# Down matrices of the expert loop loaded from ScalarE's queue in place of SyncE's

## The reference, cut to what matters

```python
# per layer: 64 experts, each token goes to 8 of them
shared = (silu(xf @ sw1) * (xf @ sw3)) @ sw2
xe = xpad[tok]                                # tokens of expert e
h  = silu(xe @ w1[e]) * (xe @ w3[e])          # w1, w3: 1024 x 256, 1 MB each
y  = (h @ w2[e]) * g[:, None]                 # w2: 256 x 1024, 1 MB
out = out.at[tok].add(y)
```

## Time and profile before

| | |
|---|---|
| time, median of 3 runs | 1429.8 us (1428.21 to 1430.89) |
| the profiled execution | 1428.44 us, of which its span is 1425.9 us |
| TensorE's granted clock, mean | 0.990 |
| busy share of the span | PE 97%, DVE 35%, ACT 24%, POOL 8% |
| HBM read | 459.52 MB |
| DMA queues | q1 (hardware) 452.07 MB, q0 (software, GpSimd's) 8.53 MB |
| expert loop, pairs 2 to 31 | about 225 to 665 us (layer 0) and 930 to 1370 us (layer 1) |

### The profile page before, as it was taken

The page is one execution under the profiler, slowest core; times in us unless marked ns, Lnnn a source line. Parts: engine busy times, 40 slices in busy tenths (PEclk is TensorE's granted clock), DMA queues, the critical chain, the costliest instruction groups (busy, mean ns, idle before and its releaser), DMA issues.

```text
span 1425.9 us, 21714 instructions
## 1 busy us (share of the span) xinstructions
PE 1383.4 (97%) x8662; PEld 852.7 (60%) x8662; DVE 503.5 (35%) x817; ACT 338.4 (24%) x860; POOL 117.7 (8%) x155
## 2 busy tenths in 40 slices
PE   9989999999999999998999999999999999999988
PEld 4555766566665666654497557656666565665543
DVE  1575623333333333334311255232333323333352
ACT  1243232222222222221110222222222222222121
POOL 1555210000000000000100133000000000000000
PEclk9989999999999999999999999999999999999999
DMA  9820449999999999998555404699999999999961
GB/s 289 290 90 1 177 184 420 421 420 421 420 421 421 421 421 420 421 420 344 186 184 176 179 0 178 271 420 421 421 421 421 421 420 422 420 422 420 421 252 59
DMA packets 80822, 461.88 MB, mean 324 GB/s; under 512 B 9184, under 2 KB 9408, under 8 KB 30560
## 3 DMA queue, kind: packets, MB, share of 16 engines
q1 hardware_dynamic: 78144, 452.07, 77.9%
q0 software_dynamic: 2592, 8.53, 2.0%
HBM read 459.52 MB, written 1.05 MB: 323 GB/s over the span
## 4 chain that ended last, share of the span: by engine, by line
PE 89%; DVE 4%; DMA 2%; issue 2%; POOL 2%; ACT 1%; SPq 0%; DVEq 0%; POOLq 0%
PE ps L1012 30%; PE ps L1040 16%; PE ps L1056 9%; PE ps L976 8%; PE ps L691 4%; PE ps L1164 4%; PE ps L872 3%; PE ps L889 2%; DMA ring<-in_exp_w_dram 2%; PE ps L917 2%; PE ps L793 1%; PE ps L857 1%; PE ps L711 1%; PE ps L926 1%; PE ps L586 1%
## 5 line engine op out<-in xcount | busy, mean ns | idle before, releaser
L1040 PE MATMUL ps<-ring,qkT 128*64 128x512 f32 x1024 | 233.8, 598 | 0.0
L1012 PE MATMUL ps<-ring,proj 128*64 128x256 f32 x2048 | 227.0, 379 | 0.3 <-DMA ring<-in_exp_w_dram 0.2
L1012 PEld LDWEIGHTS ps<-ring,proj 128*64 128x64 f32 x2048 | 147.6, 137 | 86.7 <-issue 18.2
L1799 DVE TENSOR_TENSOR o_tok<-ps,o_tok 128x1024 f32<-128x1024 f32 x124 | 151.8, 1224 | 100.4 <-PE ps L1056 100.1
L1805 DVE TENSOR_TENSOR y_lo<-ps,y_hi 128x1024 fp32r<-128x1024 f32 x62 | 76.0, 1225 | 227.6 <-ACT y_hi L1371 227.6
L1791 DVE SCALAR_TENSOR_TENSOR roped<-roped,rows,ps 128x256 f32<-128x256 f32 x64 | 30.8, 481 | 307.3 <-ACT roped L1344 299.4
L1040 PEld LDWEIGHTS ps<-ring,qkT 128*64 128x64 f32 x1024 | 67.8, 136 | 111.8 <-issue 110.4
L1012 PE MATMUL ps<-ring,pT 128*64 128x256 f32 x1024 | 121.5, 379 | 1.9 <-ACT gb_row L1338 1.9
L1012 PE MATMUL ps<-ring,gb_row 128*64 128x256 f32 x1024 | 121.4, 379 | 0.0
L1371 ACT ACTIVATE y_hi<-ps 128x1024 fp32r<-128x1024 f32 x62 | 63.5, 1024 | 223.9 <-PE ps L1040 223.9
L1056 PE MATMUL ps<-y_hi,selT 128*128 128x512 f32 x248 | 109.4, 441 | 7.4 <-DVE o_tok L1799 7.4
(11 more groups left out here) (274 smaller groups left out, 1506.3 us busy)
## 6 DMA issues: line engine op xcount, KB each, us to landing
ring<-in_exp_w_dram SPq DMA_DIRECT2D x384, 1024.0 KB, 13.8
ring<-in_od_w_in_dram SPq DMA_DIRECT2D x6, 2048.0 KB, 9.4
ring<-in_ple_w_gate_dram SPq DMA_DIRECT2D x4, 2048.0 KB, 13.1
ring<-in_ev_w_in_dram SPq DMA_DIRECT2D x3, 2048.0 KB, 18.7
ring<-in_sh_w_dram SPq DMA_DIRECT2D x6, 1024.0 KB, 7.4
ring<-in_ev_w_o_dram SPq DMA_DIRECT2D x2, 2048.0 KB, 11.0
ring<-in_od_w_o_dram SPq DMA_DIRECT2D x2, 2048.0 KB, 7.8
gb_row<-in_ln_g_dram POOLq DMA_DIRECT2D x4, 512.0 KB, 8.3
```

What stands on the lines that cost most here:

```text
L1012: ins = pe.matmul(ps[b * SLOTS:(b + 1) * SLOTS, 2, w * FE:(w + 1) * FE], xe(odd, c)[:, u * P + b * SLOTS:u * P + (b + 1) * SLOTS], views[b ...
L1040: ins = pe.matmul(ps[b * SLOTS:(b + 1) * SLOTS, 4 + half, :], hT[:, f, b * SLOTS:(b + 1) * SLOTS], views[b][:, f, half * PIECE:(half + 1) ...
L1799: dve.tensor_tensor(y_acc[:, t, :], ps[:, bank:bank + 2, :].rearrange("p b n -> p (b n)"), y_acc[:, t, :], ALU.add)\
```

## The change

SyncE's loop loses the wait for `exp_down` and the two w2 loads. ScalarE issues these two loads itself, for pair m + 2, in its step m between `y_high(m)` and `selT_copy(m + 1)`; `y_high(m)` has already waited there for `exp_down` of pair m. The loads carry the same semaphores and addresses. The number and size of all transfers stay; the loads ahead of the loop, and those after it, remain SyncE's.

```diff
                                 for v in (u, u + 1):
                                     lin_load((e0 + v) % RING, a["exp_w3"][L, i * UNROLL + v])
-                                sp.wait_ge(sem("exp_down"), i * 2 + (L * PAIRS + u // 2 - 1))
-                                for v in (u, u + 1):
-                                    down_load((e0 + v) % RING, a["exp_w2"][L, i * UNROLL + v])
...
+                def next_down(m, u):
+
+                    for v in (2 * (u % 2), 2 * (u % 2) + 1):
+                        e = 2 * m + UNROLL + v % 2
+                        src = a["exp_w2"][L, e] if isinstance(e, int) else a["exp_w2"][L, bass.ds(e, 1)]
+                        slot = (shared_item[L] + 1 + v) % RING
+                        rows_src = src.rearrange("(p c) f -> p (c f)", c=2) if isinstance(e, int) else \
+                            src.rearrange("o (p c) f -> p (o c f)", c=2)
+                        act.dma_start(ring[:, slot, DOWN0:DOWN0 + 2 * D], rows_src).then_inc(down_loaded[slot], 16)
+
...
-                def act_step(m, o, odd, u, gather_next=True, selT_next=True):
+                def act_step(m, o, odd, u, gather_next=True, selT_next=True, reload=True):
                     silu(m)
                     hT_copy(m)
                     if gather_next:
                         xe_copy(o + 1, not odd, u)
                     if selT_next:
                         y_high(m)
+                        if reload:
+                            next_down(m, u)
                         selT_copy(m + 1, 1 - u % 2)
...
                 for u in range(3):
-                    act_step(PAIRS - 4 + u, OCTETS - 1, False, u, gather_next=False)
+                    act_step(PAIRS - 4 + u, OCTETS - 1, False, u, gather_next=False, reload=u < 2)
```

## The result

The changed kernel takes 1439.51 us (median of 6, 1437.72 to 1439.94) against 1429.28 us (6 runs beside it, 1424.97 to 1431.7). The ratio is 1.0071, 95% interval 1.0054 to 1.0087: slower by some 10 us. The forecast was 1439.5.

The account below looks back on a forecast made before the run. PE and the DMA engines were taken as both full, balanced to a tenth of a microsecond. 1428.4 + 2 × 5.0 = 1438.4 us for the profiled execution; with 1.4 for the median, given as 1439.5, range 1431 to 1446.

Parts of the forecast that it names:

- What bounds the kernel: Whole loop: PE and DMA engines both full; w3's spare time falls from 6.8 us at pair 17 to nothing at pair 31.
- SP's part: SP's loop: one wait and two issues fewer per pair, w1 and w3 issued at the same moments; worth 0.
- ACT's part: Behind y_high: two more issues per pair, 0.9 us, hidden by 4.95 us of idle time before silu.
- The order: DMA queues: w2 on a second queue takes half the rate and passes w3, which lands 5.0 us later.
- What is late next: From pair 25 on, PE waits a little before each pair's w3 half and follows the full DMA engines.
- The price: Last w3 half of each layer starts 5.0 us later; both delays reach the end.
- Unchanged order: DMA queues: served in order of issue, or w2 still lands last, or unprofiled spare time is larger; 1429.8 us, chance 0.15.
- lost rate: DMA engines: alternating between queues drops them to 415 GB/s or less, 6 us more per layer; 1452 us, chance 0.12.
- late ACT: ACT's w2 issues: held up by a full queue beyond 0.9 + 4.9 us; cost 60 us at 6.8 us, chance 0.04.
- the faster case: DMA engines: two queues lift the rate and PE's waits for w3 in unprofiled runs vanish; 1427 us, chance 0.03.

Follow-up runs that it names:

- the three kernels "before" with remedies: Kernel before the change with gb_row loads after the layer's last exp_up (1427.00 us), w1 loads issued after exp_up's w1 half (1428.29), or both (1428.00).

## Why the prediction was right, point by point

**What bounds the kernel.** Right. PE and the DMA engines are both full, and the last w3 load has no spare time. Given 2.1 to 4.6 us of it (the three kernels "before" with remedies), the kernel before gains nothing that its loops show beyond 0.4 us; robbed of 5.0 us, it loses them. One reading was incomplete: the spare time does not run out by a growing backlog alone. With gb_row out of the way 2.4 us of it are left at pair 31, so that load takes about half of what is lost between pair 25 (4.5 us) and pair 31 (0.1).

**SP's part, ACT's part.** Right, both nothing. ACT's two issues took 1.26 us in the pair shown, a little over the upper end of 1.19 that I gave, under a cover of 4.2 us. They did not go out some 1 us later, behind `y_high`, but at 432.39, while `y_high` (432.25 to 433.27) still ran. The kernel with all six issues on ACT shows that they are free.

**The order.** Right, and shown by the landings, by one w2 load moved in place of two (about half of the delay) and by all six loads on ACT's one queue (no delay). w3 of pair 17 lands 4.8 us later in the span (5.0 forecast), 5.1 us later counted from the layer's first w1 half, and 23.0 us after its first issue (22 to 23). The two queues have 52 and 48 in a hundred of the engines' time while both have work, which is what the Trainium skill states in *DMA: Bandwidth & Descriptors*, "Queues, rings and completion order" (round-robin over the queues with work). By that rule, the trace agrees; its advice in "Rules for kernel authors" that a second issuing engine brings no bandwidth holds too, at 421 GB/s with one and with two.

**A size that was off.** w2 lands 13.7 to 14.2 us after issue, not 10 to 11. The 10 us for 2 MB at half rate were right; the 3.1 to 3.6 us until its first bytes move were left out. Here it cost nothing. The sum had a slip as well: 1438.4 and 1.4 make 1439.8, not 1439.5.

**What is late next.** This step failed in its shape. I had PE wait a little per pair from pair 25 on. It waits from pair 23 in layer 0 and from pair 25 in layer 1, by at most 0.5 us each, and then 3.7 and 3.9 us at pair 28, where GpSimd's gb_row loads come on a third queue. I had used that very load as evidence that another queue passes, and not asked whom it passes in the changed kernel. In the kernel before, pair 28's w3 had landed at 610.5, 8 us behind the first gb_row issue; now it is still under way then for another 7 us, and all of the 1 MB passes it. That last step is read from the landings; what is shown by a run is that with gb_row out of the way the wait is gone. In all PE's waits for expert weights came to 8.1 us, not 10.

**The price.** 5.0 us per layer was forecast; the loops lost 6.2 and 6.5. In layer 0 the wait at pair 28 is 3.7 us, the small ones from pair 23 to 27 come to some 0.9, and the lower clock behind the long wait makes 1.7; these 6.3 are the 6.2 within 0.1. The loads themselves are late by what was forecast: counted from the layer's first w1 half, pair 31's w3 lands 5.1 us later than before in layer 0 and 5.2 in layer 1. At pair 31 the w3 load lands at 639.2 + 22.9 = 662.1, about 1.2 us before PE wants it: PE had lost more than the engines asked for. That the total still came out at 10.2 us, against 10.0 forecast, is partly luck: the clock's cost in the loops, which the sum did not have, was offset by shorter low-clock stretches behind them, 2.8 us in the profiled execution.

**The rivals.** Unchanged order, lost rate, late ACT and the faster case are all refuted, by the landing times, the 421 GB/s, the kernel with everything on ACT, and the result.

## What to carry to other kernels

Where one queue carries all loads in the order of need and the DMA engines are full, a second queue is not free capacity: whatever is issued there takes half of the engines until it is through, and the first queue's loads are later by its bytes. Before moving a load, look at the spare time of the loads it will pass, at the worst place of the loop and with every other queue's traffic there, not at the mean. And with full engines a later issue costs all the time in which they run dry, once, for good, counted up to the first bytes, not up to the issue.

## What was not expected of the hardware

While the first queue is full, a load on a second, empty queue moves its first bytes 3.1 to 3.6 us after its issue (issued at 432.4, first packets between 435.5 and 436.0); where the engines were empty it took about 1.0 us (issued at 218.3 in the kernel with w2 on SP, 7 us later). A single wait of PE of 3.7 and 3.9 us within full work was followed by 3.4 us at the lower clock, in both layers of the changed kernel (PE was busy for 99.80 of the 100 us from 500 to 600). In the loops of the other kernels a wait of 2.7 us (w2 on ACT, 7 us later, layer 0) was followed by one too; a wait of 2.6 us (w2 on ACT, 10 us later, layer 0) was not. Holes of the DMA engines at the start of a loop, 3.9 us of work, show up 400 us later as a loss of 4.7 us.
